# Hybrid HGRN2 and differential-attention encoder on one core: the low parts of the weights, the exponentials' table, a store and a silu take other places in the queues of the mixers

## The chip, the cores and the metric

One core of one Trainium2 chip. The metric is the device time of the whole kernel in microseconds; less is better. The kernel is written with explicit semaphores: each engine (TensorE, VectorE, ScalarE, GpSimd, SyncE) has a program of its own that it runs strictly in order, and each wait is written by hand.

## The reference

Two sequences (256 and 512 tokens, together 768, width 1024) go through two layers. The part that matters here are the two mixers of a layer:

```python
z = rms_norm(x, norm_mix_pre[l]) @ w_in[l]          # 1024 -> 6144 columns
q_h, f_fw, f_bw, i_h, g_h, q_d, k_d, v_d, gate_a, gate_b = split(z)
a = hgrn2_mixer(q_h, f_fw, f_bw, i_h, g_h, ...)     # gated linear attention, both directions, 4 heads
b = diff_attention(q_d, k_d, v_d, ...)              # two softmaxes subtracted, with rope, 4 heads
m = sigmoid(gate_a) * (a @ w_branch_a) + sigmoid(gate_b) * (b @ w_branch_b)
x = x + rms_norm(m @ w_out, ...)
```

In the first mixer `o = rms_norm(o) * silu(g)` per head, with `q = silu(q_raw)` and forget gates from sigmoids of f. In the second `a = softmax(q1 k1) - lam * softmax(q2 k2)` per head and `a @ v`. A convolutional feed-forward block and a gated embedding follow in each layer. All is computed in float32.

## The kernel before

**Precision and units.** A float32 product is made of three fp32r matmuls: each operand is split into a high part (ScalarE's copy, `whi`, line 2463 in `high`) and a low part (VectorE's subtraction raw - high, `wlo`, line 1584 in `low`). Weights come in units of 2048 columns on 128 partitions. SP loads a unit into one of two raw buffers (`load`, line 769) after waiting (line 773) for the low part of the unit two before it, which is the last reader of that buffer. SP's queue also holds, in a fixed place behind one of those loads, the loads of Q and K for the attention of the next head (`load_qk`, line 789: one into QK at line 798 and four into QKs, the turned halves, at line 801); for the second head's successor it stands behind the load of unit 21, for the third head's behind that of unit 23. Its own waits are for the stores of these columns, for the last scores (`sc5`) and the rope of the head before.

**The mixers.** A loop over 4 heads in each of 2 layers (`mixers`, lines 1144 for TensorE, 1844 for VectorE, 2718 for ScalarE). Each head runs the gated linear attention over 7 levels of blocks (1, 2, 4 ... 64 tokens; `gla_level`, line 995), then near and far blocks, and the attention over its 6 query tiles. One iteration k of a head holds on TensorE: scores of tile k+1 (line 1089), level k (line 1018), the turning of the attention weights of tile k (line 1100), a slot of the projection z (line 1137, or 1120 for units by tokens), the values of tile k (line 1109). The projection of the later heads and gates is what fills TensorE: it is cut into parts, and `SLOTS` says how many parts each of the 13 slots of a head takes. Slot 1+k lies in iteration k; slots TAIL = 8 to 12 lie behind the levels. Where a slot holds part 1 of a unit j, `side_splits` names unit j+1: its high part is then made on ScalarE (`side` there) and its low part on VectorE (`side` here). So in a layer the units 16 and 17 are split in slots 1 and 5 of the first head, 18 in its last slot, 19 in slot 4 and 20 in slot 11 of the second, 21 in slot 3 and 22 in slot 8 of the third, 23 and 24 in slots 2 and 6 of the fourth. A finished half unit is copied out of PSUM (`copy_out`, line 2575, called by `side_out`; lines 2585 to 2590) and stored (`store_out`, line 2592); the next unit's matmuls wait for the copy.

**VectorE's order in iteration k:** keys scaled (`level_up_keys`, line 1765), maximum of the scores of tile k+1 (`att_max`, line 1827), in iteration 6 the rotation of the next head's Q and K (`att_rope`, "cqk", line 1817, which waits for `load_qk`), queries scaled (`level_up_queries`, line 1772, after TensorE's level k), for some levels the masked copy (`copy_level`, line 1795), the attention weights combined (`att_weights`, lines 1837 to 1841), and last the low part of slot 1+k. Behind the loop come row sums (line 1874), the far blocks (lines 1781, 1783), the next head's gates and keys, and `gla_output` (lines 1801, 1803), whose second copy frees the PSUM bank for the next head's diagonal (`gla_diagonal` on TensorE, line 988, first thing of the next head's work).

**ScalarE's order:** in iteration k the copy and store of `side_out(1+k)`, the attention's output (line 2751), keys merged for level k+1 (`merge_keys`, line 2544), exponentials of tile k+1 (line 2562), turned weights (line 2740), the high part; in iteration 5 both silus of the next head (`gla_silu`, lines 2524 and 2526). At a head's end: squares (lines 2806, 2808), the next head's keys, a tiny exponential that brings its table in (`exponential_table`, line 2573), the copy of slot TAIL+3 (line 2590), the diagonal's copy (`gla_diagonal`, line 2550, which level 0 of TensorE needs for its last blocks), the first exponentials, `load_v`.

Of the kernel before, what the change touches and what calls it, by code (L numbers as in the profile page):

```python
# [30 lines left out]
NH = 4  # L31
# [8 lines left out]
NL = len(LEVELS)  # L40
# [17 lines left out]
I0, I1 = 2, 14  # L58
DENSE = 15

PRE, TAIL = 0, 1 + NL
# [65 lines left out]
def view(ap, offset, dims):  # L127

    return bass.AP(tensor=ap.tensor, offset=ap.offset + offset, ap=[list(ap.ap[0])] + [list(d) for d in dims])
# [125 lines left out]
def build(nc, x_in, p_in, w_in, lb_logits, gnorm, lam_in, subln, w_a, w_b, w_out, n_mix_pre, n_mix_post,  # L255
          w_up, conv_p, w_down, n_ffn_pre, n_ffn_post, w_ple, w_ple_gate, n_ple, ident_in, masks_in,
          rope_in, out):
    with ExitStack() as ctx:
# [299 lines left out]
        def unit(L, j, i=None, each=2):  # L558

            n, half = L * N_UNITS + j, L * ((U_DN + N_UNITS - U_PG) // 2) + (j - (U_PG - U_DN if j >= U_PG else 0)) // 2  # L560
            turn = (j + L + (j >= U_PG)) % 2
            return (n, half, j % 2, turn) if i is None else (n + i * each, half + i * (each // 2), j % 2, turn)
# [966 lines left out]
        def _(dve):  # L1529
# [50 lines left out]
            def low(u):  # L1580

                n, _, s, g = u
                dve.wait_ge(w_hi, n + 1)
                v.tensor_tensor(wlo[:, g, :], raw[:, s, :], whi[:, g, :].bitcast(F32), ALU.subtract)\  # L1584
                    .then_inc(w_lo, 1)
# [258 lines left out]
            def mixers(L, h):  # L1844
                it = L * NH + h
                following = h + 1 < NH

                def side(s):
                    for j in side_splits(h, s):
                        low(unit(L, j))  # L1850

                if h == 0:
                    att_max(it, 0)
                    low(unit(L, DENSE))
                    att_weights(it, 0)
                side(PRE)
                for k in range(NL):
                    level_up_keys(it, k)
                    if k + 1 < NT:
                        att_max(it, k + 1)  # L1860
                    if following and k == NL - 1:
                        att_rope(it + 1, L, "cqk")
                    level_up_queries(it, k)
                    if k in COPIED:
                        copy_level(it, k)
                    if k == 0 and h:
                        for t in range(TAIL, len(SLOTS[h - 1])):
                            for j in side_splits(h - 1, t):
                                low(unit(L, j))
                    if k + 1 < NT:  # L1870
                        att_weights(it, k + 1)
                    side(1 + k)
                done(A_act, it, "sq")
                v.tensor_reduce(st_t[:, 0, :], SQ2, AX_X, ALU.add).then_inc(*A_dve.step("ss"))
                if following:
                    att_rope(it + 1, L, "sqk")
                far_up(it)
                if following:
                    att_rope(it + 1, L, "radd")
                    gla_forget(it + 1)  # L1880
                done(A_pool, it, "rs")
                v.tensor_tensor(O2[:], O2[:], view(st_t[:], 2 * NT, [[1, NT], [0, P]]), ALU.mult).then_inc(*A_dve.step("on"))
                if following:
                    gla_keys(it + 1)
                    att_low(it + 1)
                gla_output(it)
                if following:
                    att_max(it + 1, 0)
                done(G_pool, it, "rs")
                done(G_out, it, "o")  # L1890
                v.tensor_tensor(O1, O1, view(st_g[:], 2 * NT, [[1, NT], [0, P]]), ALU.mult).then_inc(*G_out.step("on"))
                if following:
                    gla_queries(it + 1)
                else:
                    done(A_pe, it, "tro1")
                for k, n in ((0, 4), (1, 2)):
                    done(G_tro, it, f"tro{k}")
                    cols = slice(4 * k * P, (4 * k + n) * P)
                    v.scalar_tensor_tensor((ab1 if following else abT[:, NH - 1, :])[:, cols], ps[:, (AB[2], GB[0])[k], 0:n * P], gn_col[:],
                                           gT[:, it % 2, cols], ALU.mult, ALU.mult).then_inc(*G_out.step(f"ab{k}"))  # L1900
                if following:
                    att_weights(it + 1, 0)
                if not following:
                    for s in range(TAIL, len(SLOTS[h])):
                        side(s)

            for L in range(DEPTH):
# [78 lines left out]
                for i in range(2):  # L1986
                    it = L * 2 + i
# [326 lines left out]
                following = L + 1 < DEPTH  # L2314
# [18 lines left out]
                following = L + 1 < DEPTH  # L2333
# [118 lines left out]
        def _(act):  # L2452
# [67 lines left out]
            def gla_silu(it):  # L2520
                act.wait_ge(s_fz, it * 16 + 16)
                if it:
                    done(G_pe, it - 1, "diag")
                a(Qb[:], FZ[:, 0, :], ACT.Silu).then_inc(*G_gate.step("silu_q"))
                act.wait_ge(s_g, it * 16 + 16)
                a(gT[:, it % 2, :], gT[:, it % 2, :], ACT.Silu).then_inc(*G_gate.step("silu_g"))

            def gla_sigmoids(it):
                if it:
                    done(G_dve, it - 1, "uq0")  # L2530
                    done(G_tot, it - 1, "tot1")
                a(F[:], FZ[:, 1:3, :], ACT.Sigmoid).then_inc(*G_gate.step("sig"))
# [13 lines left out]
            def gla_diagonal(it):  # L2546
                if it:
                    done(G_out, it - 1, "ss")
                done(G_pe, it, "diag")
                a(AT[:], view(ps[:], GB[1] * 512 + 256, [[P, NT], [1, P]]), ACT.Copy).then_inc(*G_act.step("dg"))  # L2550
# [19 lines left out]
            def exponential_table(it):  # L2570
                if it:
                    done(A_table, it - 1, "in")
                a(exp_ahead[:], half_neg[:, 0:1], ACT.Exp).then_inc(*A_table.step("in"))
# [144 lines left out]
            def mixers(L, h):  # L2718
                it = L * NH + h
                following = h + 1 < NH  # L2720

                def side_out(s):
                    for j, b in side_halves(h, s):
                        copy_out(L, j, b, (6, 7))
# [5 lines left out]
                def side(s):  # L2730
                    for j in side_splits(h, s):
                        high(unit(L, j))
# [8 lines left out]

                if h == 0:
                    gla_diagonal(it)
                side(PRE)
                for k in range(NL):
                    side_out(1 + k)
                    if k:
                        if k == 1:
                            act.wait_ge(ab_st[1], heads_stored(L, h))
                        done(A_pe, it, f"av{k - 1}")  # L2750
                        a(O2[:, k - 1, :], ps[:, AB[2], 0:P], ACT.Identity, scale=rc[:, (k - 1) % 2, 0:1]).then_inc(*A_act.step(f"oc{k - 1}"))
                    if k == 0:
                        turned_weights(0)
                    if k + 1 < NL:
                        merge_keys(it, k + 1)
                    side_store(1 + k)
                    if k + 1 < NT:
                        att_exponentials(it, k + 1)
                    if 0 < k < NT:
                        turned_weights(k)  # L2760
                    side(1 + k)
                    if following and k == 2:
                        load_qf(L, h + 1)
                    if following and k == 5:
                        gla_silu(it + 1)
                    if not following and k == 5:
                        done(A_pe, it, f"sc{NT - 1}")
                        act.wait_ge(ab_st[0], heads_stored(L, h))
                        load_ab(0, NH - 1)
# [36 lines left out]
                a(SQ1[:, 4:NT, :], view(ps[:], GB[1] * 512, [[P, NT - 4], [1, P]]), ACT.Square).then_inc(*G_sq.step("sq1"))  # L2806
                done(G_out, it, "o0")
                a(SQ1[:, 0:4, :], view(ps[:], GB[0] * 512, [[P, 4], [1, P]]), ACT.Square).then_inc(*G_sq.step("sq"))
                if following:
                    merge_keys(it + 1, 0)  # L2810
                exponential_table(it)
                side(TAIL + 2)
                side_out(TAIL + 3)
                if following:
                    gla_diagonal(it + 1)
                    att_exponentials(it + 1, 0)
# [84 lines left out]
            for L in range(DEPTH):  # L2901
# [44 lines left out]
                for e in range(I0, I1):  # L2946
# [25 lines left out]
                    if e == I0 + 6:  # L2972
                        done(in_row_lo, L, "%s_%d" % TURNED[-1])
                        load_qk(L, 0)
                gla_silu(L * NH)
                gla_sigmoids(L * NH)
                gla_sigmoid_neg(L * NH)
                in_copy(L, I1 - 1, "c21")
# [7 lines left out]
                done(lay_dve, L, "slw")  # L2986
                merge_keys(L * NH, 0)
                copy_out(L, I1, 1, (6, 7))
                store_out(L, I1, 1)
                for h in range(NH):  # L2990
                    mixers(L, h)
                for c in range(KD // 2, KD):
# [5 lines left out]
                for i in range(2):  # L2998
                    it = L * 2 + i
# [485 lines left out]
```

## Time and profile before

| what | us |
|---|---|
| three runs: median (lowest, highest) | 2416.17 (2415.14, 2419.05) |
| the profiled execution | 2415.63 |
| its span from first to last instruction | 2413.7 |
| TensorE busy, share of the span | 2401.1, 99% |
| VectorE busy | 1839.3, 76% |
| ScalarE busy | 1311.3, 54% |
| GpSimd busy | 197.1, 8% |
| granted TensorE clock, mean | 0.999 of full speed |

The mixers of the first layer lie at about 236 to 500 us of the span, those of the second at 1432 to 1696; in these stretches TensorE is busy for 262.4 and 261.7 us of 264. In the rows, a line starts with the start time and the duration, then engine, line of the kernel, operation, written and read tiles, shapes and a count; in brackets stands how long the engine had been idle and what ended that. Ends of matmuls are modelled. Tile names are those of the memory: several logical tiles share one place, so a row may show AX, KM or FZ for data that the code calls by another name (O1 shows as AX, SQ1 and SQ2 as AT and At).

### The profile page before, as it was taken

What the parts mean: (1) busy time and instruction counts of PE and PEld (TensorE: products, weight loads), DVE (VectorE), ACT (ScalarE), POOL (GpSimd) and SP (SyncE); (2) the same over time, 40 slices, a digit from 0 to 9 for tenths busy, and PEclk for the clock granted to TensorE, in tenths of its full rate; (3) what the DMA queues carried; (4) which work ended last, traced back from release to release, by engine and by line L of the source; (5) the groups of instructions that cost most, each with busy time, mean ns of one, the idle gap of its engine ahead of it and who ended that gap; (6) DMA issues with size and microseconds to landing.
All of it is one profiled execution on the core that took longest, in us unless ns stands there. A gap on an engine that the chain in (4) does not pass through costs nothing.

```text
span 2413.7 us, 40388 instructions
## 1 busy us (share of the span) xinstructions
PE 2401.1 (99%) x16188; PEld 2241.4 (93%) x16188; DVE 1839.3 (76%) x2412; ACT 1311.3 (54%) x2022; POOL 197.1 (8%) x236
## 2 busy tenths in 40 slices
PE   9999999999999999999999999999999999999998
PEld 8999999998999999888889999999989999998887
DVE  7666788764888999978585568887649889999784
ACT  6445666542555556456464456664426555554563
POOL 1001011100200000003110011111001000000031
PEclk9999999999999999999999999999999999999999
DMA  5454444353323233733233544434443233346421
GB/s 178 136 175 141 137 146 136 126 181 133 103 89 92 83 97 121 289 123 122 98 131 129 186 136 141 138 129 143 159 150 105 65 90 93 104 164 241 160 89 62
DMA packets 284667, 320.97 MB, mean 133 GB/s; under 512 B 10433, under 2 KB 216769, under 8 KB 284482
## 3 DMA queue, kind: packets, MB, share of 16 engines
q1 hardware_dynamic: 211680, 171.39, 22.8%
q10 hardware_dynamic: 72802, 147.01, 16.8%
q8 instruction: 129, 2.11, 0.4%
q14 instruction: 56, 0.46, 0.1%
HBM read 253.08 MB, written 65.27 MB: 132 GB/s over the span
## 4 chain that ended last, share of the span: by engine, by line
PE 94%; DVE 3%; ACT 1%; issue 1%; DMA 0%; SPq 0%; DVEq 0%; ACTq 0%; POOLq 0%; POOL 0%
PE ps L909 23%; PE ps L1192 14%; PE ps L1397 13%; PE ps L1137 8%; PE ps L882 6%; PE ps L1503 5%; PE ps L1120 3%; PE ps L1366 3%; PE ps L1333 3%; PE ps L896 3%; PE ps L1252 3%; PE ps L961 1%; PE ps L1483 1%; PE ps L1109 1%; PE ps L1089 1%; PE ps L1018 1%
## 5 line engine op out<-in xcount | busy, mean ns | idle before, releaser
L2143 DVE TENSOR_TENSOR wlo<-raw,whi 128x1024 fp32r<-128x1024 f32 (+1 forms) x152 | 163.8, 1079 | 55.1 <-ACT whi L3165 55.1
L909 PE MATMUL ps<-hT_hi,whi 128*128 128x384 f32 x608 | 203.1, 334 | 0.0
L909 PE MATMUL ps<-hT_hi,wlo 128*128 128x384 f32 x608 | 203.1, 334 | 0.0
L909 PE MATMUL ps<-hT_lo,whi 128*128 128x384 f32 x608 | 203.1, 334 | 0.0
L3179 ACT ACTIVATE U<-ps 128x384 f32<-128x384 f32 x152 | 74.8, 492 | 223.2 <-PE ps L909 223.2
L1397 PE MATMUL ps<-whi,PH_hi 128*128 128x512 f32 x456 | 179.0, 393 | 0.0
L1397 PE MATMUL ps<-whi,PH_lo 128*128 128x512 f32 x456 | 177.6, 390 | 0.0
L1397 PE MATMUL ps<-wlo,PH_hi 128*128 128x512 f32 x456 | 177.5, 389 | 0.0
L1584 DVE TENSOR_TENSOR wlo<-raw,whi 128x2048 fp32r<-128x2048 f32 x53 | 121.3, 2288 | 64.8 <-ACT whi L2463 64.8
L1711 DVE TENSOR_TENSOR wlo<-raw,whi 128x1024 fp32r<-128x1024 f32 (+1 forms) x98 | 102.8, 1069 | 79.3 <-ACT whi L2637 79.2
L909 PE MATMUL ps<-S_hi,whi 128*128 128x384 f32 x456 | 152.3, 334 | 0.0
L909 PE MATMUL ps<-S_hi,wlo 128*128 128x384 f32 x456 | 152.3, 334 | 0.0
L909 PE MATMUL ps<-S_lo,whi 128*128 128x384 f32 x456 | 152.3, 334 | 0.0
L3165 ACT ACTIVATE whi<-raw 128x1024 fp32r<-128x1024 f32 (+1 forms) x152 | 142.1, 937 | 15.3 <-PE ps L961 14.8
L1137 PE MATMUL ps<-hT_hi,whi 128*128 128x384 f32 x512 | 137.1, 348 | 1.6 <-ACT hn L2590 1.2
L3102 ACT ACTIVATE PH_hi<-prod 128x768 fp32r<-128x768 f32 (+1 forms) x82 | 65.2, 798 | 129.4 <-PE ps L1397 107.1
L1137 PE MATMUL ps<-hT_lo,whi 128*128 128x384 f32 x512 | 130.5, 335 | 0.0
L1137 PE MATMUL ps<-hT_hi,wlo 128*128 128x384 f32 x512 | 130.4, 335 | 0.0
L1192 PE MATMUL ps<-IS_hi,whi 128*128 128x384 f32 x384 | 128.3, 334 | 0.0
L1192 PE MATMUL ps<-IS_hi,wlo 128*128 128x384 f32 x384 | 128.3, 334 | 0.0
L1192 PE MATMUL ps<-IS_lo,whi 128*128 128x384 f32 x384 | 128.3, 334 | 0.0
L2463 ACT ACTIVATE whi<-raw 128x2048 fp32r<-128x2048 f32 x53 | 101.5, 1914 | 37.9 <-PE ps L896 19.9
(348 smaller groups left out, 6940.1 us busy)
## 6 DMA issues: line engine op xcount, KB each, us to landing
raw<-w_up_dram SPq DMA_DIRECT2D x88, 512.0 KB
raw<-w_in_dram SPq DMA_DIRECT2D x62, 512.0 KB
raw<-w_down_dram SPq DMA_DIRECT2D x60, 512.0 KB, 4.5
raw<-w_in_dram SPq DMA_DIRECT2D x16, 1024.0 KB
zT<-gst ACTq DMA_DIRECT2D x40, 384.0 KB, 2.4
GT<-zT ACTq DMA_DIRECT2D x16, 768.0 KB, 5.7
pD<-CG ACTq DMA_DIRECT2D x26, 384.0 KB, 2.3
zT<-hn ACTq DMA_DIRECT2D x48, 192.0 KB, 1.9
```

The lines of the kernel that those rows point to most:

```text
L882: ins = mm(ps[:, bank, c0:c0 + TH], W[b][:, s, w0:w0 + P], rhs[a][:, k, th * TH:(th + 1) * TH], start=(i == 0), stop=(i == n - 1))
L909: ins = mm(ps[:, 4 * (j % 2) + bank, 0:TH], quarter(L, W[y], j, (w,))[:, 0, k * P:(k + 1) * P], sum_operand(a, x, k), start=(opens and k = ...
L1137: ins = mm(ps[:, bank, c0:c0 + TH], W[y][:, w[3], w0:w0 + P], hT[x][:, k, th * TH:(th + 1) * TH], start=(k == 0 and i == 0), stop=(k == KD ...
L1192: ins = mm(ps[:, 4 * (e % 2) + bank, 0:TH], in_quarter(L, W[y], e, (w,))[:, 0, k * P:(k + 1) * P], in_operand(a, x, k), start=(opens and k ...
L1397: ins = mm(ps[:, FIRST_BANK[q] + t, :], ph_slot(a, n)[:, k, t * P:(t + 1) * P], view(W[b][:], ring_at(L, n) + k * 512, [[1, 512]]), start= ...
L1503: ins = mm(ps[:, t, :], gate_tokens(a, 4 * u + k, t), W[b][:, w[3], k * 512:(k + 1) * 512], start=(u == 0 and k == 0 and q == 0), stop=(u ...
L1584: v.tensor_tensor(wlo[:, g, :], raw[:, s, :], whi[:, g, :].bitcast(F32), ALU.subtract)\
L1711: v.tensor_tensor(in_quarter(L, wlo, e, names), in_raw(e, names), in_quarter(L, whi, e, names).bitcast(F32), ALU.subtract)\
L2143: v.tensor_tensor(lo, x, hi.bitcast(F32), ALU.subtract)\
L2463: a(whi[:, g, :], raw[:, s, :], ACT.Copy).then_inc(w_hi, 1)
L3165: a(hi, x, ACT.Copy).then_inc(*((w_hi, 1) if part == "T3N4" else q_hi.step(f"{part}{j}")))
L3179: a(dst, ps[:, bank + (2 if name == "p5" else 0), 0:TH], ACT.Copy).then_inc(*q_act.step(f"{name}_{j}"))
```

## The change

Four moves; no instruction is added or taken away.

1. VectorE: in iterations 1 to 6 the low part of slot k is made after the level's masked copy and before the attention weights; before, it was made at the end of iteration k-1. That of slot 7 would follow the loop (no unit is split there).
2. ScalarE, at the end of a head: the exponentials' table and the copy of slot TAIL+3 come ahead of the next head's merged keys.
3. ScalarE, at the start of the first head: the store of the second half of unit 14 comes behind the diagonal's copy.
4. ScalarE: the silu of the gate moves from the end of iteration 5 to iteration 6, behind the copy of slot 7.

```diff
@@ VectorE, mixers
                         for t in range(TAIL, len(SLOTS[h - 1])):
                             for j in side_splits(h - 1, t):
                                 low(unit(L, j))
+                    elif k:
+                        side(k)
                     if k + 1 < NT:
                         att_weights(it, k + 1)
-                    side(1 + k)
+                side(NL)
                 done(A_act, it, "sq")
@@ ScalarE, gla_silu
                 a(Qb[:], FZ[:, 0, :], ACT.Silu).then_inc(*G_gate.step("silu_q"))
+
+            def gla_silu_gate(it):
                 act.wait_ge(s_g, it * 16 + 16)
                 a(gT[:, it % 2, :], gT[:, it % 2, :], ACT.Silu).then_inc(*G_gate.step("silu_g"))
@@ ScalarE, mixers
                 if h == 0:
                     gla_diagonal(it)
+                    store_out(L, I1, 1)
                 side(PRE)
                 for k in range(NL):
                     side_out(1 + k)
+                    if following and k == NL - 1:
+                        gla_silu_gate(it + 1)
@@
                 a(SQ1[:, 0:4, :], view(ps[:], GB[0] * 512, [[P, 4], [1, P]]), ACT.Square).then_inc(*G_sq.step("sq"))
+                exponential_table(it)
+                side_out(TAIL + 3)
                 if following:
                     merge_keys(it + 1, 0)
-                exponential_table(it)
                 side(TAIL + 2)
-                side_out(TAIL + 3)
@@ ScalarE, ahead of the heads
                 gla_silu(L * NH)
+                gla_silu_gate(L * NH)
@@
                 copy_out(L, I1, 1, (6, 7))
-                store_out(L, I1, 1)
                 for h in range(NH):
                     mixers(L, h)
```

## Rows read from the trace of the kernel before

**Rows 1.** The page's chain that ended last, by engine.

```profile
PE 94%; DVE 3%; ACT 1%; issue 1%; DMA 0%; SPq 0%; DVEq 0%; ACTq 0%; POOLq 0%; POOL 0%
```

**Rows 2.** Waits of TensorE, whole span: us in total, times, longest us.

```profile
PE ps L1137 <- ACT hn L2590: 1.2, 4, 0.4
...
PE ps L1018 <- ACT AT L2550: 0.8, 2, 0.4
PE ps L1109 <- ACT At L2740: 0.7, 2, 0.4
...
PE ps L1137 <- ACT gst L2590: 0.4, 2, 0.2
```

**Rows 3.** Timeline, start of the first head, layer 0: ScalarE, TensorE.

```profile
244.22 0.81 ACT L2550 ACTIVATE AT<-ps 128x768 f32<-128x768 f32 x1 [0.44 <-ACT gst L2588]
...
245.08 0.37 PE L1018 MATMUL ps<-QP,KM 128*32 128x32 f32 x16 [0.35 <-ACT AT L2550]
```

**Rows 4.** Timeline of ScalarE, the gate's silu at the first head's end.

```profile
284.51 0.83 ACT L2526 ACTIVATE gT<-gT 128x768 f32<-128x768 f32 x1
```

**Rows 5.** Timeline, end of the third head, layer 0: ScalarE, TensorE.

```profile
425.91 1.20 ACT L2544 ACTIVATE KM<-KS 128x768 f32<-128x768 f32 x1
...
428.53 0.79 ACT L2590 ACTIVATE hn<-ps 128x768 f32<-128x768 f32 x1
...
429.38 0.44 PE L1137 MATMUL ps<-hT_hi,whi 128*128 128x384 f32 x1 [0.43 <-ACT hn L2590]
```

**Rows 6.** Timeline, fourth head, iterations 1 and 2: VectorE, TensorE.

```profile
447.17 2.29 DVE L1584 TENSOR_TENSOR wlo<-raw,whi 128x2048 fp32r<-128x2048 f32 x1 [0.88 <-ACT whi L2463]
...
452.67 0.33 PE L1137 MATMUL ps<-hT_hi,wlo 128*128 128x384 f32 x1
452.84 0.51 PE L1137 MATMUL ps<-hT_lo,whi 128*128 128x384 f32 x2
453.72 0.71 PE L1109 MATMUL ps<-vD,At 128*128 128x128 f32 x4 [0.36 <-ACT At L2740]
```

**Rows 7.** Timeline, second head, iterations 4 to 6, layer 0: VectorE, TensorE, SyncE's queue.

```profile
334.13 2.29 DVE L1584 TENSOR_TENSOR wlo<-raw,whi 128x2048 fp32r<-128x2048 f32 x1 [1.08 <-ACT whi L2463]
335.52 0.39 PE L1089 MATMUL ps<-QK_hi,QK_lo 64*128 64x512 f32 x2
336.51 0.39 SPq L777 DMA_DIRECT2D raw<-w_in_dram  x1
337.10 0.41 SPq L798 DMA_DIRECT2D QK<-zT  x1
337.21 1.22 DVE L1827 TENSOR_REDUCE mx<-ps 128x2 f32<-128x1024 f32 x1
...
347.39 1.76 DVE L1817 TENSOR_TENSOR QK<-QK,rope 128x1536 f32<-128x1536 f32 x1 [2.82 <-DMA QKs<-zT]
```

**Rows 8.** Timeline, second head's end, layer 0, and the same rotation in layer 1.

```profile
349.29 0.96 DVE L1772 TENSOR_TENSOR QP<-QP,TOT 128x768 f32<-128x768 f32 x1
...
362.31 0.41 DVE L1803 COPY AX<-ps 128x256 f32<-128x256 f32 x1
362.87 0.62 PE L988 MATMUL ps<-Qb,KM 128*32 128x32 f32 x48
...
1545.09 1.76 DVE L1817 TENSOR_TENSOR QK<-QK,rope 128x1536 f32<-128x1536 f32 x1 [3.48 <-DMA QKs<-zT]
```

**Rows 9.** DMA view, 330 to 352 us: 40 slices' rate; issues with size, us to landing.

```profile
GB/s 56 0 0 0 0 0 0 0 0 30 0 0 0 32 173 296 380 387 374 395 411 408 425 413 223 201 246 240 207 302 302 97 0 0 0 0 0 0 0 0
...
zT<-hn ACTq DMA_DIRECT2D x1, 384.0 KB, 5.7
```

**Rows 10.** Timeline of VectorE, third head, iteration 6, layer 0.

```profile
412.28 0.96 DVE L1772 TENSOR_TENSOR QP<-QP,TOT 128x768 f32<-128x768 f32 x1 [2.43 <-PE ps L1018]
```

**Rows 11.** Timeline, fourth head behind its levels, layer 0: VectorE, TensorE.

```profile
478.03 0.94 DVE L1874 TENSOR_REDUCE st_t<-At 128x6 f32<-128x768 f32 x1
...
481.73 0.60 PE L1039 MATMUL ps<-ident,KS 128*128 128x128 f32 x4
```

## The prediction

> **What bounds the kernel now.** I read the page first: the chain that ended last is 94% TensorE, with 3% on VectorE and 1% on ScalarE [rows 1]. So only time in which TensorE stands still can be won, and only work that makes it stand still can be lost. Next the waits of TensorE. The reader is to see how little is there: for copies out of PSUM (into hn or gst) 1.2 us in four waits and 0.4 us in two, for the diagonal's copy 0.8 us in two, for the turned attention weights 0.7 us in two [rows 2]. That is 3.1 us in ten waits, and the four edits touch just these. What the table doesn't show is where VectorE and its transfers run without slack beside TensorE, so I went through the timeline of the heads, engine by engine, in the order of the edits.
>
> A printed wait is short of the true loss, since a matmul's modelled end lies past the point where the next one could start. A matmul of 384 columns is drawn 0.33 us long, but the next one starts after 0.17 (452.67, 452.84). After the two from 452.84 on, whose row lasts 0.51, the next could start at 453.19, and it starts at 453.72: 0.53 us lost where 0.36 is printed [rows 6]. Waits behind small matmuls lose less, by my estimate 0.07 to 0.2 us each over the print. For ten waits I add 1.0 us: 4.1 us in all, bounds 3.1 and 4.7.
>
> **Part 1: the diagonal's copy ahead of a store** (first head of each layer). ScalarE idles 0.44 us between the projection's copy and the diagonal's copy, because the store waits for the first and is issued there; TensorE gets its level 0 going again at 245.08, when the diagonal's copy ends [rows 3]. The store moves behind the copy, costs its issue later, where ScalarE next waits for TensorE anyway, and lands under a microsecond later; the next user of that buffer is a whole block away. Worth the 0.44 and a little more, 0.5 us a layer: -1.0 us.
>
> **Part 2: table and filler copy ahead of the keys** (head ends). Before, the keys' copy (1.20 us) and the table come ahead of the projection's copy, which starts at 428.53, lasts 0.79, and TensorE goes on at 429.38 [rows 5]. After, the copy can start when its matmuls end and is over before the diagonal and first scores are through. The same happens with a smaller wait at the end of the first head. I take 0.5 and 0.25 us, twice: -1.5 us, of the six waits for projection copies [rows 2]. What comes later is the keys' copy, by the 0.79 of the filler copy and what the filler waits for, and behind it the diagonal's copy, the first exponentials and the load of the values, all about 0.7 us; level 0, which wants keys and diagonal, comes only behind another slot of projection and the turned outputs. Cost nil under that cover, 0.7 us a head without it.
>
> **Part 3: the gate's silu behind a copy.** The silu of the gate lasts 0.83 us [rows 4] and stands ahead of the copy for which TensorE waits at the end of the first head's levels; the wait is at most 0.4 us [rows 2], so it goes whole. The gate is wanted a head later. Twice 0.25: -0.5 us. The rest of ScalarE's work there comes no later, as the two only change places.
>
> **Part 4: low parts one slot later.** Six subtractions of 2.29 us a layer (units 16, 17, 19, 21, 23, 24) move from the end of one iteration behind the level's copy of the next. In the fourth head the subtraction at 447.17 held up keys, maximum, exponentials and turned weights, and TensorE waited at 453.72 [rows 6]; now the maximum goes first. -0.53 twice: -1.1 us. In exchange the weights' scaling of that iteration comes up to 2.3 us later. TensorE wants it only in the next iteration, behind a slot of projection, the values and the next scores: cost nil under that cover, and at most the 2.3 us of one part where it is gone.
>
> In the fourth head unit 24's part now comes ahead of the row sums at 478.03. The subtraction's 2.29 and the sums' 0.94 from there end near 481.2, the short update of the far keys follows them, and TensorE turns those keys at 481.73 [rows 11]. It just fits; I take nothing, bound 0.5.
>
> **The cost that the edit doesn't show** is on SP's queue. In the second head the subtraction ran at 334.13; it frees the raw buffer, so SP issues the load of w_in at 336.51, and only behind it, in its own order, the loads of Q and K for the next head from 337.10 on [rows 7]. VectorE then idles 2.82 us before the rotation of those keys, at 347.39, until they land [rows 7], and 3.48 us in layer 1 [rows 8]. So these loads already set when the rotation starts. In the new order the part waits for the maximum, which waits for the scores: they end at 335.91, maximum 1.22, queries 0.96 (each starts about 0.1 before the last one ends), so the subtraction starts near 337.95 instead of 334.13: 3.8 us later, and the loads with it [rows 7].
>
> The rotation is ahead of the level's queries on VectorE. Before, it ended 0.15 us ahead of the queries at 349.29, and from there VectorE's timeline has fourteen rows with no idle time printed on any, the first at 349.29 and the last the copy at 362.31, whose end lets TensorE start the next diagonal at 362.87, within 0.15 us [rows 8]. That run of some 13 us has no slack, neither before nor after. Layer 0: 3.8 less the 0.2 between rotation and queries, +3.6 us. Layer 1, where the queries were already waiting for the rotation: +3.8 us. Both ends: nothing, if the loads weren't what the rotation waits for; 4.8 a layer, if the landing moves further than its issue (rival 2). I take 3.6 and 3.8, because idle time put down to that very DMA stands on both rows.
>
> In the third head the same load of w_in (unit 23) now slides to just before Q and K, which wait for the scores there. Behind the rotation, up to the queries at 412.28, VectorE waits 2.43 us for TensorE [rows 10]; sharing the transfers' time may take 1.3 to 2.0 of it. It holds. First head: Q and K come ahead of unit 19's load, no change.
>
> **Sum.** -1.0 -1.5 -0.5 -1.1 +3.6 +3.8 = +3.3 us. The profiled execution took 2415.63 (span 2413.7 and 1.9 around it), so 2418.9; the median of the runs is 0.54 above that execution, so 2419.5.
>
> **Where page and trace could part.** The store of hn in this stretch took 5.7 us from issue to landing, with SP's loads issued before it, though 384 KB at the 387 GB/s of a busy slice is 1.0 us [rows 9]. It waited behind the loads. The Trainium skill, DMA: Bandwidth & Descriptors, section "Queues, rings and completion order", says that an SDMA engine takes turns between the queues that have work, a packet at a time. By that rule a store that meets the loads at their start would share their time: the sum would then be +5.3. The trace doesn't bear out an even share, as this store came last.
>
> **Rivals.**
> 1. *The landing doesn't move* (the loads are held by something else, or the moved part is early enough). Then only the gains count: 2416.17 - 4.1 = 2412.1. For: the transfers run at their rate whenever they start. Against: SP issues within 0.1 us of the subtraction's end, and VectorE's idle time ends with the DMA. Chance 0.13.
> 2. *Slower than before*: the store of hn (issued at a time that TensorE sets) now falls together with the start of the w_in load and gets ahead of Q and K. 0.384 MB at 387 GB/s: 1.0 us on the landing, twice, so +5.3 and 2421.5. It decides from a landing 0.8 us a layer later than I take. For: the store's issue stays while the loads slip 3.8 us. Against: it was served last before. Chance 0.16.
> 3. *Half of it*: the landing moves, but by some 2 us, as loads that no longer start in the middle of the level's other traffic run faster; -4.1 + 3.8 = -0.3, 2415.9. The rates of the slices speak little for it. Chance 0.10.
> My forecast has 0.61, with its own range 2417.5 to 2421.2.
>
> **Numbers.** A difference of under 0.2% (4.8 us) can't be told from none in this kernel; so 2411.3 and 2421.0 are the bounds. Slower: a tenth of the forecast's 0.61 and two thirds of rival 2's 0.16, 0.18 with what I haven't seen. Faster: only if rival 1 holds and every gain is at its upper bound, 0.03. Same: 0.79. The range takes in the forecast, most of rivals 2 and 3, and stops short of rival 1: 2413.5 to 2422.5.
>
> **What would show it.** Right: TensorE's waits for hn, gst, AT and At all but gone; new waits, about 2.3 us at the near level of the second head (queries of L1772) and the rest up to 3.6 at its turned outputs and next diagonal (copy L1803); VectorE idle some 7 us before the second head's rotation; SP's loads there issued 3.8 us later against the scores. Wrong: that rotation starts as early as before against TensorE's work, the diagonal follows without a wait, and the time falls by 4; or TensorE waits for transposed weights, which would mean that part 4's cover is gone.

## The result, and the profile after

| | before | after |
|---|---|---|
| median, us (7 runs each, beside each other) | 2418.63 | 2425.91 |
| lowest to highest, us | 2415.14 to 2419.05 | 2422.89 to 2426.88 |
| the profiled execution, us (span) | 2415.63 (2413.7) | 2425.91 (2424.0) |

The ratio is 1.0033, with an interval of 1.0024 to 1.0042: the change makes the kernel 0.33% or 7.3 us slower. Forecast were +3.3 us on a base of 2416.17, so 2419.5, and "same". The profiled executions lie 10.3 us apart, of which 2.3 us arise in the first 12 us, ahead of all edited code (last section); so the parts below are taken from where the same matmul starts in the two traces, from the first head on.

The page after, the chain that ended last:

```profile
PE 98%; DMA 1%; DVE 0%; issue 0%; SPq 0%; ACT 0%; DVEq 0%; POOLq 0%; POOL 0%; ACTq 0%
```

VectorE's 3% and ScalarE's 1% of the chain [rows 1] are gone and 1% of DMA has come: the path runs through a transfer now. The waits of TensorE after, whole span (us in total, times, longest us):

```profile
PE ps L1029 <- DVE QP L1772: 8.3, 2, 4.8
PE ps L858 <- DVE gst L1544: 1.0, 1, 1.0
PE ps L1397 <- issue: 0.6, 1, 0.6
PE ps L976 <- ACT X L2896: 0.4, 1, 0.4
```

All ten waits that the edits were aimed at [rows 2] are gone. In their place stand two, one in the second head of each layer, for the queries of the near level. (L858 lies ahead of the heads, L976 and L1397 outside the edited code.)

Where that wait comes from, in the timeline after of the second head, layer 0, of VectorE and SyncE's queue:

```profile
337.29 1.23 DVE L1827 TENSOR_REDUCE mx<-ps 128x2 f32<-128x1024 f32 x1 [2.05 <-PE ps L1089]
338.43 0.95 DVE L1772 TENSOR_TENSOR QP<-QP,TOT 128x768 f32<-128x768 f32 x1
339.30 2.29 DVE L1584 TENSOR_TENSOR wlo<-raw,whi 128x2048 fp32r<-128x2048 f32 x1
...
341.67 0.39 SPq L777 DMA_DIRECT2D raw<-w_in_dram  x1
342.25 0.42 SPq L798 DMA_DIRECT2D QK<-zT  x1
342.72 1.95 SPq L801 DMA_DIRECT2D QKs<-zT  x4
...
353.65 1.76 DVE L1817 TENSOR_TENSOR QK<-QK,rope 128x1536 f32<-128x1536 f32 x1 [7.75 <-DMA QKs<-zT]
355.33 0.95 DVE L1772 TENSOR_TENSOR QP<-QP,TOT 128x768 f32<-128x768 f32 x1
```

This answers to [rows 7]. The low part now comes behind maximum and queries; w_in is issued at its end and Q and K behind that; and the rotation waits 7.75 us for them where it waited 2.82. TensorE in the same stretch:

```profile
352.34 0.51 PE L1137 MATMUL ps<-hT_lo,whi 128*128 128x384 f32 x2
356.33 2.32 PE L1029 MATMUL ps<-QP,KS 128*128 128x128 f32 x12 [3.48 <-DVE QP L1772]
358.30 0.99 PE L1137 MATMUL ps<-hT_hi,whi 128*128 128x384 f32 x2
359.09 0.84 PE L1137 MATMUL ps<-hT_hi,wlo 128*128 128x384 f32 x2
...
360.76 0.51 PE L1137 MATMUL ps<-hT_hi,wlo 128*128 128x384 f32 x2
```

Pairs of matmuls of the same shape take 0.51 us ahead of the wait, 0.84 to 0.99 behind it, and 0.51 again from 360.76. The view by stretches (us, TensorE busy, granted clock, share of the DMA engines, GB/s) names the reason:

```profile
350.00:356.00 6.00, 2.85 (x32) 1.00 0.36 92
356.00:360.00 4.00, 3.67 (x17) 0.63 0.00 0
360.00:364.00 4.00, 4.00 (x31) 0.94 0.01 2
```

The granted clock drops behind the standstill of 3.48 us. In the records it is at half (1.2 of 2.4 GHz) for 3.4 us; in layer 1 it is so for 6.8 us, about a standstill of 4.79 us. So the late queries are paid for twice.

The DMA view after, 334 to 356 us (answers to [rows 9]; issues with size and us to landing):

```profile
QKs<-zT SPq DMA_DIRECT2D x4, 192.0 KB, 8.8
QK<-zT SPq DMA_DIRECT2D x1, 768.0 KB, 8.1
zT<-hn ACTq DMA_DIRECT2D x1, 384.0 KB, 8.1
```

Before, the store of hn took 5.7 us [rows 9], and the two loads:

```profile
QK<-zT SPq DMA_DIRECT2D x1, 768.0 KB, 6.7
QKs<-zT SPq DMA_DIRECT2D x4, 192.0 KB, 7.8
```

All three share the stretch now, and all three take longer.

Added up by the offset of TensorE's work against before (us, after less before):

| stage | layer 0 | layer 1 |
|---|---|---|
| first head (parts 1 to 3) | -0.99 | -1.01 |
| second head, near level | +3.65 | +4.95 |
| second head, half clock | +1.72 | +2.11 |
| second head's diagonal, end of third head | -0.67 | -1.09 |
| fourth head (part 4) | -0.64 | -0.66 |
| net | +3.1 | +4.3 |

Together 7.4, as the medians say. (Of the 10.3 us between the profiled executions, 0.6 more arise at the matmuls of L1397, far behind the mixers; its idle time of 0.6 is put down to "issue" and stands in some kernels' traces and not in others, whatever their edit.) The fourth row holds the third head's gain (-0.48 and -0.47) and -0.19 and -0.62 from waits that went. The second head costs 5.2 us in layer 0 (3.65 + 1.72 - 0.19) and 6.4 in layer 1; the gains are 2.1 us a layer.

### The profile page after: what moved, and what is told of

Same layout as the page of the kernel before. It is cut to its first block, busy times and chain, and to the rows that moved or that the text cites. A ratio compares the mean times of both kernels' runs of the same rounds, so it can differ in the third digit from the quotient of the medians.

```text
span 2424.0 us, 40388 instructions
## 1 busy us (share of the span) xinstructions
PE 2406.4 (99%) x16188; PEld 2246.0 (93%) x16188; DVE 1836.6 (76%) x2412; ACT 1311.3 (54%) x2022; POOL 197.3 (8%) x236
## 3 DMA queue, kind: packets, MB, share of 16 engines
q8 instruction: 129, 2.11, 0.4%
## 4 chain that ended last, share of the span: by engine, by line
PE 98%; DMA 1%; DVE 0%; issue 0%; SPq 0%; ACT 0%; DVEq 0%; POOLq 0%; POOL 0%; ACTq 0%
PE ps L909 23%; PE ps L1192 14%; PE ps L1397 13%; PE ps L1137 10%; PE ps L882 6%; PE ps L1503 5%; PE ps L1120 3%; PE ps L1366 3%; PE ps L1333 3%; PE ps L896 3%; PE ps L1252 3%; PE ps L1089 2%; PE ps L961 1%; PE ps L1483 1%; PE ps L1109 1%; PE ps L1018 1%
## 5 line engine op out<-in xcount | busy, mean ns | idle before, releaser
L1397 PE MATMUL ps<-whi,PH_hi 128*128 128x512 f32 x456 | 179.0, 393 | 0.6 <-issue 0.6
L1397 PE MATMUL ps<-whi,PH_lo 128*128 128x512 f32 x456 | 177.6, 390 | 0.0
L1397 PE MATMUL ps<-wlo,PH_hi 128*128 128x512 f32 x456 | 177.5, 389 | 0.0
```

The costliest lines, as they stand in the source:

```text
L1397: ins = mm(ps[:, FIRST_BANK[q] + t, :], ph_slot(a, n)[:, k, t * P:(t + 1) * P], view(W[b][:], ring_at(L, n) + k * 512, [[1, 512]]), start= ...
```

## The experiments

Eight kernels were run, and two of the kernels once more. Each ratio is against the kernel before, run beside it. "Rotation late" is the start of the second head's rotation against the start of TensorE's last level there, compared with the same distance before: it shows how far the loads slid.

**Which of the moved parts costs: unit 19 alone.** First everything of the change but that part, which stays where it was:

```diff
+                    elif k and (h, k) != (1, 4):
                         side(k)
                     if k + 1 < NT:
                         att_weights(it, k + 1)
+                    if (h, k) == (1, 3):
+                        side(4)
```

> The changed kernel, with one low part put back: unit 19's, in the second head, is made at the end of iteration 3 as before; the five others stay one slot later. Theory (that one part delays the loads of w_in, Q and K behind it on SP's queue, and all of the loss comes from there): no wait of TensorE at L1029, the second head's rotation (L1817) no later against TensorE's work than before, and the gains of the four parts left alone: 4.2 us faster than before (3.5 to 4.5), 11 to 12 us faster than the changed kernel. Rival (the moved low parts or the reordered ScalarE work cost as a whole): the wait at L1029 stays, or the time is within 1 us of before or above it.

2414.27 us (2410.89 to 2415.38) against 2417.89: ratio 0.9986, 0.9977 to 0.9995. The medians give 3.6 us, TensorE's offsets 4.1. No wait for queries is left in the list of TensorE's waits, and the rotation there starts as early against TensorE's work as before (within 0.15 us), with the old idle time:

```profile
348.87 1.76 DVE L1817 TENSOR_TENSOR QK<-QK,rope 128x1536 f32<-128x1536 f32 x1 [2.80 <-DMA QKs<-zT]
```

Then the converse, the kernel before with only that part moved:

```diff
+                    if (h, k) == (1, 4):
+                        side(4)
                     if k + 1 < NT:
                         att_weights(it, k + 1)
-                    side(1 + k)
+                    if (h, k) != (1, 3):
+                        side(1 + k)
```

> The kernel before, with one thing of the change: unit 19's low part in the second head made behind the queries of iteration 4. Theory: TensorE waits 3.5 and 4.8 us at L1029 in the two layers, its clock falls to half for some 3 and 7 us behind it, and the kernel is 11.6 us slower than before (10 to 12.5), less the 0.2 and 0.6 us that TensorE waited before at the next diagonal. Rival (the loss needs the other moves as well): under 6 us slower.

2429.69 us (2428.38 to 2430.81), 11.8 above the kernel before: ratio 1.0051, 1.0038 to 1.0063. Its waits of TensorE:

```profile
PE ps L1029 <- DVE QP L1772: 8.8, 2, 5.2
PE ps L1137 <- ACT hn L2593: 1.2, 4, 0.4
...
PE ps L1018 <- ACT AT L2553: 0.8, 2, 0.4
PE ps L1109 <- ACT At L2743: 0.7, 2, 0.4
```

The waits that the edits were aimed at all stand, and the new one beside them. Both kernels say the same: the whole loss is unit 19's subtraction, and the rest of the change is worth about 4 us.

**Is it the place of the loads, not of the subtraction?** All low parts moved as in the change, but SyncE issues the loads of Q and K for the third and fourth head ahead of the load of w_in that waits for the freed buffer:

```diff
                 for j, (h, u) in enumerate(IN_UNITS):
+                    if j in (DENSE + 6, DENSE + 8):
+                        load_qk(L, 2 if j == DENSE + 6 else 3)
...
-                    for head in range(1, NH):
-                        first = SIDE_STARTS[head - 1] + sum(SLOTS[head - 1][:5])
-                        if j == min(DENSE + (first - 2) // 8 + 3, N_IN - 1):
-                            load_qk(L, head)
+                    if j == DENSE + 3:
+                        load_qk(L, 1)
```

> The changed kernel, with SP issuing the loads of Q and K for the third and fourth heads ahead of the load of w_in behind which they stood (of units 21 and 23). Theory: Q and K of the third head are then bound by the scores alone, are issued some 4 us earlier, the rotation waits for nothing or less than before, no wait at L1029, and besides the 4.2 us of the four parts the 0.2 and 0.6 us waited before at the second head's end are gone: 4 to 5 us faster than before, 11 to 12 faster than the changed kernel. Rival (the low part's place on VectorE is what costs, not SP's order): the wait at L1029 stays above 2 us.

2413.47 us (2410.44 to 2415.4), 4.4 below before: ratio 0.9980, 0.9971 to 0.9989. Its timeline, SyncE's queue and VectorE:

```profile
334.87 0.37 SPq L798 DMA_DIRECT2D QK<-zT  x1
...
339.12 0.42 SPq L777 DMA_DIRECT2D raw<-w_in_dram  x1
...
343.25 1.75 DVE L1817 TENSOR_TENSOR QK<-QK,rope 128x1536 f32<-128x1536 f32 x1
```

The rotation runs without idle time ahead of it, 2.9 to 3.6 us earlier against TensorE's work than before the change. With the subtraction still late, the loss is gone: it was the order of one queue. The same order in the kernel before:

> The kernel before, with SP's loads of Q and K for the third and fourth heads ahead of the loads of units 21 and 23, and nothing else. Theory: the second head's rotation waits less or not, the two waits at its end (0.2 and 0.6 us) go, 0.8 us faster than before and at most 1; so nearly all that the changed kernel gains with this order comes from its own four parts. Rival (the order of the loads is worth more by itself): over 2 us faster.

(the edit is the one above, on the kernel before.) 2417.55 us, ratio 0.9998, 0.9989 to 1.0007: no difference that can be told. By the trace it wins 0.5 us of the expected 0.8, in layer 1, where TensorE waited for the diagonal's copy. The early landing is no gain by itself; it pays for the delay of the subtraction.

**The store beside the loads.** In the second head, the store of hn that met the loads is issued behind the near block's copies:

```diff
-                    side_store(1 + k)
+                    if (h, k) != (1, 5):
+                        side_store(1 + k)
...
+                if h == 1:
+                    side_store(6)
                 side_store(TAIL)
```

> The changed kernel, with the store of the half unit in slot 6 of the second head issued behind the near blocks' copies, so that it doesn't meet the loads of w_in, Q and K. Theory A (the store's packets share the engines with the loads and hold Q and K up by 1.1 and 1.7 us beyond the later issue): issue to landing of QKs falls from 8.8 us to about 7.7, the rotation comes 1 us earlier against TensorE's work in each layer, the wait at L1029 falls to 2.4 and 3.2 us, and the kernel is 2 to 3 us faster than the changed one, more if the clock then stays at full speed. Theory B (the store is served behind the loads, as before, and the landing is late for another reason, such as the small packets of the loads themselves): no change of the rotation, within 0.5 us of the changed kernel.

2420.76 us (2419.54 to 2424.49), ratio 1.0017, 1.0008 to 1.0026: 5.2 below after and 2.9 above before. Not all of the 5.2 is the store's: by TensorE's offsets the two second heads cost 3.0 us less than in after, and the profiled executions lie 3.3 us apart; the rest fits the two groups of the last section. The loads now land as soon after their issue as before the change, layer 0:

```profile
QK<-zT SPq DMA_DIRECT2D x1, 768.0 KB, 6.8
QKs<-zT SPq DMA_DIRECT2D x4, 192.0 KB, 7.7
```

This kernel and after were executed once more, unchanged, to see what varies between executions:

> The changed kernel once more, for the landing of Q and K. With the store on time the second head's rotation came later than before, against TensorE's work, by 4.9 to 5.1 us in layer 0 (three executions) and by 4.0 to 5.9 in layer 1. Theory A (the store beside the loads costs): again over 4.7 in layer 0. Rival (chance between executions): 4.3 or less.

> The changed kernel with the second head's store of slot 6 issued late, once more. Theory A: again 4.1 to 4.4 us in layer 0, and 4.1 to 4.6 in layer 1. Rival: 4.7 or more in layer 0.

They took 2426.31 and 2421.37 us. For every second head, in us: how late the rotation is, how long TensorE then stood still at L1029, how long the records show half clock behind that, and what the head cost by TensorE's offsets:

| | late | standstill | half clock | cost |
|---|---|---|---|---|
| after, layer 0 | 4.94 | 3.48 | 3.4 | 5.2 |
| after again, layer 0 | 5.01 | 3.55 | 3.4 | 5.3 |
| only unit 19 moved, layer 0 | 5.03 | 3.57 | 3.4 | 5.3 |
| store late, layer 0 | 4.21 | 2.75 | none | 4.0 |
| store late again, layer 0 | 4.06 | 2.59 | 3.4 | 4.4 |
| after, layer 1 | 5.59 | 4.79 | 6.8 | 6.4 |
| after again, layer 1 | 5.26 | 4.46 | 6.8 | 6.6 |
| only unit 19 moved, layer 1 | 6.01 | 5.22 | 6.8 | 7.4 |
| store late, layer 1 | 4.16 | 3.36 | 3.4 | 4.6 |
| store late again, layer 1 | 6.05 | 5.25 | 3.4 | 6.4 |

In layer 0 three executions with the store in place agree within 0.1 us, and the store's removal brings 0.8 to 0.9 us; 0.3 to 0.4 us of lateness beyond the issue's 3.8 stay even so, and their cause is open. In layer 1 one and the same kernel scatters by 1.9 us (store late: 4.16 and 6.05, where 4.1 to 4.6 was expected), and what the store costs there stays open. The traces show where much of the scatter arises: in SyncE's own issues. In layer 1 the issue of QK takes 1.22 us in after, where it takes 0.42 in a kernel whose rotation is only 4.00 late (the filled one, below). After, then the filled one:

```profile
1542.33 1.22 SPq L798 DMA_DIRECT2D QK<-zT  x1
...
1542.81 0.42 SPq L798 DMA_DIRECT2D QK<-zT  x1
```

From the start of that issue to the end of the fourth of QKs it is 3.7 us in after and 2.5 in the filled kernel, 4.0 and 4.4 in the two executions that are over 6 us late, and 2.4 in layer 0 of after. Why an issue takes longer there is not shown.

Less lateness also meant a shorter standstill. The second head of store late, layer 0, first execution and then the second:

```profile
353.08 1.76 DVE L1817 TENSOR_TENSOR QK<-QK,rope 128x1536 f32<-128x1536 f32 x1 [7.03 <-DMA QKs<-zT]
...
355.76 1.64 PE L1029 MATMUL ps<-QP,KS 128*128 128x128 f32 x12 [2.75 <-DVE QP L1772]
...
352.53 2.93 PE L1029 MATMUL ps<-QP,KS 128*128 128x128 f32 x12 [2.59 <-DVE QP L1772]
```

In the first the twelve matmuls take 1.64 us where they took 2.32: the clock stayed at 2.4 GHz. In the second they take 2.93 us at 1.2 GHz, though the standstill was shorter.

**The clock by itself.** The change, with 20 further matmuls of 384 columns into a bank that is overwritten before anyone reads it, put where TensorE stood still:

```diff
+                if h == 1:
+                    for _ in range(20):
+                        mm(ps[:, GB[2], 0:TH], hT_hi[:, 0, 0:P], hT_hi[:, 0, 0:TH], start=True, stop=True)
                 gla_near(it)
```

> The changed kernel, with 20 more matmuls of 384 columns on TensorE ahead of the near blocks of each second head, into a PSUM bank that the near blocks overwrite: 3.5 us of work inside the wait for the queries. The landing of Q and K and VectorE's run to the next diagonal stay as they are. Theory (TensorE's clock falls to half because it stood still, and that costs 0.5 and 0.9 us beyond the late transfers): the wait at L1029 shrinks to under 0.5 and some 1.3 us, the granted clock stays at full speed, matmuls behind it take 111 ns each and not 213, and the kernel is 1.3 us faster than the changed one. Rival (the extra time is VectorE's, not the clock's): full clock and no change of the time, or slower.

2422.67 us (2420.24 to 2425.36), ratio 1.0022, 1.0013 to 1.0031: 3.2 below after, with more work to do. Timeline of TensorE, layer 0:

```profile
353.50 3.63 PE L1171 MATMUL ps<-hT_hi 128*128 128x384 f32 x20
357.28 1.64 PE L1029 MATMUL ps<-QP,KS 128*128 128x128 f32 x12 [0.15 <-DVE QP L1775]
358.67 0.59 PE L1137 MATMUL ps<-hT_hi,whi 128*128 128x384 f32 x2
```

The near level and the projection behind it run at full clock, in both layers. The rotation of layer 0 came 5.08 us late, 0.14 more than in after, and the second head cost 4.8 us instead of 5.2: the clock's share is about 0.5 us in layer 0. In layer 1 this execution's loads landed sooner (rotation 4.0 us late), so the kernel's 3.2 us are not all the clock's. There the share is worked out: VectorE's unbroken run carries a delay of the rotation through to the diagonal, as the prediction had it. At full clock that holds (here the head of layer 1 cost 4.0 us at 4.0 late); in after the rotation is 5.6 late and the head cost 6.4, so 0.9 us come on top, and 1.3 and 1.4 in the other two executions with half clock for 6.8 us. At full clock TensorE also waits where the prediction had put the rest of the loss, at the diagonal (L988, once in each layer):

```profile
PE ps L988 <- DVE AX L1806: 1.6, 2, 0.8
```

**What the gains hang on.** The three moves on ScalarE alone, no low part moved:

> The kernel before with the three moves on ScalarE (store behind the diagonal's copy, table and filler copy ahead of the keys, gate's silu behind a copy) and none of the low parts moved. Theory (each move takes away its own wait and nothing else): TensorE's waits for hn, gst and AT gone, the two for At (0.53 us each) still there, 3.1 us faster than before. With the kernel that keeps unit 19's part in place, this gives the five other low parts 1.1 us. Rival (a part of the ScalarE moves costs elsewhere): under 2 us faster.

(the edit is points 2 to 4 of the change.) 2414.42 us (2412.98 to 2416.5) against 2417.92: ratio 0.9989, 0.998 to 0.9997. The medians give 3.5 us, but by TensorE's offsets the mixers gain 1.6 (0.94 and 0.69 in the two layers), not 3.1. The list of waits names what took the rest:

```profile
PE ps L1109 <- ACT At L2742: 1.7, 2, 0.9
...
PE ps L988 <- DVE AX L1803: 0.8, 1, 0.8
```

The wait for turned weights in the fourth head was 0.7 in two [rows 2]; it has grown by what the third head's end gains, 1.0 us in all. Another 0.3 go at the diagonal in layer 1 (0.8 for 0.6). ScalarE and VectorE don't hang on TensorE there, so TensorE only comes earlier to the same date. Then the same with unit 23's low part one slot later, as the only one:

```diff
+                    if (h, k) == (3, 2):
+                        side(2)
                     if k + 1 < NT:
                         att_weights(it, k + 1)
-                    side(1 + k)
+                    if (h, k) != (3, 1):
+                        side(1 + k)
```

> The kernel before with the three moves on ScalarE and one of the six low parts one slot later: unit 23's, in the fourth head. Theory (of the six moves that of unit 23 gives the whole gain, that of 19 the whole loss, and the other four lie beside other work): as the kernel that only leaves unit 19's part in place, 4 us faster than before, within 0.7 us of it; the waits for At gone. It should beat the kernel with the ScalarE moves alone by some 2 us and not by the 1.1 of my prediction, since there the fourth head's waits for At had grown from 0.7 to 1.7 us. Rival (the other four parts help too, or cost): more than 1 us away from the kernel that keeps unit 19's part.

2411.41 us (2410.91 to 2414.29) against 2417.81: ratio 0.9981, 0.9972 to 0.999. Its waits of TensorE, all of them:

```profile
PE ps L858 <- DVE gst L1544: 1.0, 1, 1.0
PE ps L988 <- DVE AX L1803: 0.4, 1, 0.4
PE ps L976 <- ACT X L2897: 0.4, 1, 0.4
```

By TensorE's offsets it gains 2.06 and 2.2 us in the two layers, as the kernel that kept only unit 19 in place does (2.1 and 2.0). So of the six moved low parts unit 23's brings all that the six bring, unit 19's brings the loss, and the other four bring nothing that can be told (0.2 us between the two kernels). This kernel and the one with Q and K ahead both beat the kernel before, by 0.19% and 0.20% in the ratios; the two can't be told apart.

## Why the prediction was wrong

**The base.** The forecast of 2419.5 stands on 2416.17, the median of the first three runs; the seven that ran beside the change have 2418.63, since a kernel's times fall in two groups (last section). Of the 6.4 us between forecast and result, 2.5 are this, and the rest is +7.3 in place of +3.3.

**The gains: right.** Parts 1 to 4 were put at -4.1 us; TensorE's offsets give -4.2. By heads: at the start of the first head 0.5 forecast and 0.47 measured in both layers (part 1); the first head's end 0.25 + 0.25 forecast (parts 2 and 3), 0.52 and 0.54 measured; the third head's end 0.5, 0.48 and 0.47; the fourth head 0.53, 0.64 and 0.66. What the prediction missed is that the third head's gain is not part 2's own: without part 4 it ends in the fourth head's wait. Its sum was right only because both were in the change.

**The mechanism of the loss: right.** Low part behind the scores, raw buffer freed later, loads of Q and K behind w_in in SyncE's order, rotation and queries late, no slack up to the diagonal: every step is in the timeline, and taking the loads out of that order takes the loss away. The issue moved as far as forecast: the low part was put near 337.95 on the clock of before, and starts at 339.30 in a trace that is 1.32 us late there, which makes 337.98.

**The size: the step that failed** is the term of the late loads of Q and K, "+3.6 us" and "+3.8 us", 7.4 in all. The second heads cost 5.2 and 6.4 us, 11.6 in all. Two things lie between:

1. The landing moved further than the issue: the rotation is 4.9 us late in layer 0 and 5.6 in layer 1, against 3.8 of the issue. Rival 2 had that place (it priced 4.8) and the right cause: the store of hn, no longer last, runs beside the loads (8.1 us to its landing, Q and K 8.1 and 8.8 for 6.7 and 7.8). Issued later, it gives back 0.8 to 0.9 us in layer 0, and the loads land in 6.8 and 7.7 us again. The prediction held against this that the store came last before. That row was about another arrival: the store was issued 5.2 us behind the load of Q and K then (342.29 for 337.10), and 1.4 behind it now (343.61 for 342.25), since TensorE's work sets its time. The rule that it set beside it (the Trainium skill, DMA: Bandwidth & Descriptors, section "Queues, rings and completion order": an engine takes turns between the queues that have work, packet by packet) agrees with the trace after: QK lands at 350.4, the store at 351.7 and the last of QKs at 353.6, so the queue that began later did not wait for the other to end. For layer 1 the traces don't separate the store's share from a scatter of 2 us, much of which lies in SyncE's slower issues (1.22 us for QK instead of 0.42).
2. The clock. No step, bound or rival held that TensorE, after standing still, goes on at half speed. It adds some 0.5 us in layer 0 (shown by the filled kernel) and 0.9 in layer 1 (worked out).

**Where the wait would stand: half right.** "About 2.3 us at the near level" and the rest at the diagonal was forecast; there were 3.48 and 4.79 at the near level and none at the diagonal. At the near level the wait is the forecast 2.3 plus the 1.1 by which the landing moved further (4.9 for 3.8). The rest, 1.3 us by the forecast, would have been due at the diagonal; but half clock held TensorE back by 1.72 us before it got there, so it came later than VectorE's copy. Where the clock stayed full, in both heads of the filled kernel and in layer 0 of store late, the wait at the diagonal is there, with 0.8 us.

**The third head: no wait, as said, but with less room.** Sharing was to take 1.3 to 2.0 of the 2.43 us [rows 10]. Timeline of VectorE after:

```profile
416.95 1.76 DVE L1817 TENSOR_TENSOR QK<-QK,rope 128x1536 f32<-128x1536 f32 x1 [2.85 <-DMA QKs<-zT]
418.81 0.96 DVE L1772 TENSOR_TENSOR QP<-QP,TOT 128x768 f32<-128x768 f32 x1
```

The rotation would be over at 418.71 and the queries start at 418.81: next to nothing is left. Some 2.3 us of slack are used, more than the forecast's 2.0, and still TensorE does not wait.

**Unit 24 "just fits": right.** Timeline of VectorE and TensorE after, fourth head (answers to [rows 11]):

```profile
483.45 2.28 DVE L1584 TENSOR_TENSOR wlo<-raw,whi 128x2048 fp32r<-128x2048 f32 x1
485.65 0.95 DVE L1876 TENSOR_REDUCE st_t<-At 128x6 f32<-128x768 f32 x1
486.51 0.42 DVE L1781 TENSOR_TENSOR KS<-KS,TOT 128x256 f32<-128x256 f32 x1
...
487.16 0.60 PE L1039 MATMUL ps<-ident,KS 128*128 128x128 f32 x4
```

The far keys are ready at 486.93, 0.2 us ahead of the matmuls that turn them.

**Rivals.** 1 and 3 (no or half a shift) fall: the rotation moved by more than its loads. Rival 2 holds for layer 0, but its price missed the clock. "Idle some 7 us before the rotation" was right (7.75 and 9.06).

## What to carry to other kernels

When a step moves, follow what its end releases through the issuing queue: everything behind it in order slides too, and a load that an idle engine already waits for pays in full. Put loads whose data is wanted first ahead of a load that waits for a buffer; here that swap turned +0.33% into -0.20%. A wait of some us in a saturated TensorE can cost more than its length (nine of ten here ended in half clock), and a gain ahead of another engine's fixed date is no gain until that date moves too.

## What the hardware showed beyond that

**Half clock after a standstill.** TensorE stood still at L1029 for 2.59 to 5.25 us in the ten second heads of the table above. Behind nine of them the records show 1.2 GHz, for 3.4 us in six and 6.8 in three; matmuls of L1029 come every 213 ns then, against 111. The length of the standstill doesn't say which it will be: behind 2.75 us the clock stayed at 2.4 GHz and behind 2.59 it fell; 4.46 us brought 6.8 us of half clock and 5.25 only 3.4.

**The start differs between executions.** TensorE reaches its full pace at different work in the two profiled executions, though nothing was edited there. TensorE before, then after:

```profile
4.16 1.98 PE L864 MATMUL ps<-wrows,gst 1*128 1x512 f32 x4
...
6.07 3.08 PE L858 MATMUL ps<-gst 128*128 128x128 f32 x18
```

```profile
4.33 3.78 PE L864 MATMUL ps<-wrows,gst 1*128 1x512 f32 x4
...
8.03 4.21 PE L858 MATMUL ps<-gst 128*128 128x128 f32 x18
```

Four matmuls of 512 columns take 1.98 us in one and 3.78 in the other. The view of the granted clock doesn't show it (1.00 for that stretch in both), so that the clock is the reason is read from the pace alone. The same 22 matmuls end 3.1 us later (12.24 for 9.15), of which 2.3 are left at the first head. The times of most of the kernels timed here fall in two groups 2.3 to 3 us apart, which fits this. Of the twelve profiled executions, six reach the first head within 0.6 us of the kernel before and six 2.3 to 3.1 us later; the executions without a profile can't be looked into. A median over few runs can sit in either group, so for differences under 3 us the offsets inside the trace were read, not the medians.
